# Rotating queries and keys before their norm is applied, and taking squares and weighted copies tile by tile from the accumulation banks, in a decoder step on one Trainium2 core

## The reference, cut to what matters

```python
def rms_norm(x, gain=None):
    x32 = x.astype(jnp.float32)
    y = x32 * lax.rsqrt(jnp.mean(x32 * x32, axis=-1, keepdims=True) + EPS)
    if gain is not None:
        y = y * gain.astype(jnp.float32)
    return y.astype(x.dtype)

def rope_partial(x, pos):
    ...
    x1, x2 = x32[..., :half], x32[..., half:ROPE_DIM]
    out = jnp.concatenate([x1 * cos - x2 * sin, x1 * sin + x2 * cos, x32[..., ROPE_DIM:]], axis=-1)

def qkv_heads(h, pos, w_qkv, q_gain, k_gain):
    qkv = (h @ w_qkv).reshape(Bt, S, N_GROUPS, 3, N_HEADS, HEAD_DIM)
    q = rope_partial(rms_norm(qkv[:, :, :, 0], q_gain), pos)
    k = rope_partial(rms_norm(qkv[:, :, :, 1], k_gain), pos)
    return q, k, qkv[:, :, :, 2]
```

## Time and profile before

| | us |
|---|---|
| median of 3 runs | 2579.95 (2577.85 to 2580.0) |
| the profiled execution's own time | 2578.79 |
| its span, first to last instruction | 2577.0 |
| TensorE matmul busy in it | 2436.4 (95%) |
| VectorE busy | 1443.5 (56%) |
| ScalarE busy | 956.0 (37%) |
| GpSimd busy | 631.1 (24%) |

### The profile page before, as it was taken

The page is one execution under the profiler, slowest core; times in us unless marked ns, Lnnn a source line. Parts: engine busy times, 40 slices in busy tenths (PEclk is TensorE's granted clock), DMA queues, the critical chain, the costliest instruction groups (busy, mean ns, idle before and its releaser), DMA issues.

```text
span 2577.0 us, 51040 instructions
## 1 busy us (share of the span) xinstructions
PE 2436.4 (95%) x19172; PEld 2200.3 (85%) x19172; DVE 1443.5 (56%) x3329; ACT 956.0 (37%) x1564; POOL 631.1 (24%) x445
## 2 busy tenths in 40 slices
PE   7888999999999999999789978899899999999998
PEld 2577888888889999999687345699899999999998
DVE  5674269467878433333534132259988996333333
ACT  3333433333333444444322021254444443444443
POOL 1014457400000222222243000267800001222222
PEclk8899999999999999999899989899999999999999
DMA  6514445544544454554623563344433333544444
GB/s 242 189 69 145 139 164 190 179 164 158 170 165 138 155 182 163 166 168 163 219 99 106 203 240 125 123 142 163 139 130 124 130 130 131 182 166 166 163 164 139
DMA packets 114388, 405.45 MB, mean 157 GB/s; under 512 B 13240, under 2 KB 13368, under 8 KB 113112
## 3 DMA queue, kind: packets, MB, share of 16 engines
q1 hardware_dynamic: 110616, 388.68, 44.6%
q10 hardware_dynamic: 3648, 15.08, 1.5%
HBM read 394.58 MB, written 9.14 MB: 157 GB/s over the span
## 4 chain that ended last, share of the span: by engine, by line
PE 67%; issue 21%; POOL 9%; DVE 1%; ACT 1%; DMA 1%; POOLq 0%; ACTq 0%; DVEq 0%; SPq 0%
PE ps L1254 11%; PE ps L1250 11%; PE ps L1258 11%; POOL ring_lo L1892 8%; PE ps L1113 7%; PE ps L1114 7%; PE ps L1117 7%; PE ps L1185 5%; PE ps L925 2%; PE ps L701 1%; POOL ring_lo L1899 1%; PE ps L705 1%; PE ps L708 1%; PE ps L777 1%; PE ps L935 1%
## 5 line engine op out<-in xcount | busy, mean ns | idle before, releaser
L364 ACT ACTIVATE wt_hi<-ring 128x1024 fp32r<-128x1024 f32 x552 | 580.4, 1051 | 681.3 <-PE ps L1117 408.5
L1841 DVE TENSOR_TENSOR ring_lo<-ring,wt_hi 128x1024 fp32r<-128x1024 f32 x256 | 315.3, 1232 | 494.7 <-ACT wt_hi L364 494.7
L1113 PE MATMUL ps<-split,wt_hi 128*128 128x288 f32 x2048 | 574.2, 306 | 2.8 <-ACT big L415 2.0
L1114 PE MATMUL ps<-split,wt_hi 128*128 128x288 f32 x2048 | 560.9, 298 | 0.0
L1918 POOL TENSOR_TENSOR split<-big,split 128x288 fp32r<-128x288 f32 x256 | 209.7, 819 | 1261.4 <-ACT split L465 664.2
L1113 PEld LDWEIGHTS ps<-split,wt_hi 128*128 128x128 f32 x2048 | 387.4, 189 | 18.6 <-issue 13.3
L1114 PEld LDWEIGHTS ps<-split,wt_hi 128*128 128x128 f32 x2048 | 387.9, 189 | 0.3
L1117 PE MATMUL ps<-split,ring_lo 128*128 128x288 f32 x2048 | 315.4, 296 | 9.8 <-POOL ring_lo L1892 9.5
L1892 POOL TENSOR_TENSOR ring_lo<-ring,wt_hi 128x1024 fp32r<-128x1024 f32 x104 | 283.2, 2731 | 146.6 <-ACT wt_hi L364 146.3
L1250 PE MATMUL ps<-split,wt_hi 128*128 128x288 f32 x2048 | 313.3, 295 | 5.7 <-DVE ada L1559 3.2
L1254 PE MATMUL ps<-split,wt_hi 128*128 128x288 f32 x2048 | 313.8, 295 | 0.0
(11 more groups left out here) (299 smaller groups left out, 2353.8 us busy)
## 6 DMA issues: line engine op xcount, KB each, us to landing
ring<-in_stream SPq DMA_DIRECT2D x680, 512.0 KB, 3.3
big<-in_kc SPq DMA_DIRECT2D x8, 1792.0 KB, 9.1
big<-in_vc SPq DMA_DIRECT2D x14, 1024.0 KB, 5.9
out_qk<-big ACTq DMA_DIRECT2D x1, 3456.0 KB, 13.0
x_spill<-xT ACTq DMA_DIRECT2D x2, 1152.0 KB, 5.0
big<-x_spill ACTq DMA_DIRECT2D x2, 1152.0 KB, 6.0
out_v<-big ACTq DMA_DIRECT2D x1, 1536.0 KB, 15.9
xT<-in_xT SPq DMA_DIRECT2D x1, 1152.0 KB, 11.1
```

Of the source, the lines that this page charges most:

```text
L364: nc.scalar.activation(wt_hi[:, n % 2 if b is None else b], ring[:, n % RING], ACT.Copy).then_inc(S["hi_ready"], 1)
L1113: mm(out, w, h_hi[:, c], start=(c == 0), stop=False)
L1114: mm(out, w, h_lo[:, c], start=False, stop=False)
L1841: TT(ring_lo[:, s], ring[:, s], wt_hi[:, s % 2].bitcast(F32), ALU.subtract)\
```

## The change

The order of the steps is turned round. ScalarE now takes each tile from its bank as soon as it is made, in two instructions: a copy into `qk` that multiplies by the gain on the way, and a square into `asq`. TensorE waits for the square of one tile, not for the copy of a group, before it writes that bank again. The rotation is applied to the weighted copy, before the norm's factor is known; its product with the sines goes into a buffer of its own, `turned_qk`, so that `asq` stays with the squares. The factor is multiplied in last. `rotate` stands behind tile 0 of the next group, `norm` behind tile 1, `spread_out` behind tile 3.

```diff
                     act.wait_ge(S["tile_done"], QK + 4 * gs + m + 1)
-                    if gs < 5 or m < 2:
+                    nc.scalar.activation(qk[:, 4 * gs + m, :], ps[:, m, 0:T], ACT.Copy, scale=(kg if gs % 2 else qg))\
+                       .then_inc(S["aq_copied"], 1)
+                    if gs and m == 0:
+                        high(act, QK + 4 * gs + 2)
+                        act.wait_ge(S["aq_ms"], gs)
+                    nc.scalar.activation(asq[:, m, :], ps[:, m, 0:T], ACT.Square).then_inc(S["aq_sq"], 1)
+                    if (gs < 5 or m < 2) and (gs == 0 or m):
                         high(act, QK + 4 * gs + m + 2)
-                    if gs and m == 0:
+                    if gs and m == 1:
                         qk_root(gs - 1)
-                nc.scalar.activation(qk[:, 4 * gs:4 * gs + 4, :], ps[:, 0:4, 0:T], ACT.Copy)\
-                   .then_inc(S["aq_copied"], 1)
...
             def norm(gs):
-                pe.wait_ge(S["aq_sq"], gs + 1)
-                if gs:
-                    pe.wait_ge(S["aq_done"], gs)
+                pe.wait_ge(S["aq_sq"], 4 * gs + 4)
+                pe.wait_ge(S["aq_turned"], gs + 1)
...
             def rotate(gs):
-                pe.wait_ge(S["aq_qn"], gs + 1)
+                if gs == 0:
+                    pe.wait_ge(S["in_att"], 80)
+                pe.wait_ge(S["aq_copied"], 4 * gs + 4)
+                if gs:
+                    pe.wait_ge(S["aq_done"], gs)
...
             for gs in range(6):
-                if gs:
-                    pe.wait_ge(S["aq_copied"], gs)
                 for m in range(4):
+                    if gs:
+                        pe.wait_ge(S["aq_sq"], 4 * gs + m - 3)
                     qk_tile(4 * gs + m, ps[:, m, 0:T])
                     if gs and m == 0:
+                        rotate(gs - 1)
+                    if gs and m == 1:
                         norm(gs - 1)
-                    if gs and m == 1:
+                    if gs and m == 3:
                         spread_out(gs - 1)
-                    if gs and m == 2:
-                        rotate(gs - 1)
...
-            pe.wait_ge(S["aq_copied"], 6)
+            pe.wait_ge(S["aq_sq"], 24)
...
-            def finish(gs):
+            def turn_qk(gs):
                 q = qk[:, 4 * gs:4 * gs + 4, :]
                 v.wait_ge(S["aq_rot"], gs + 1)
-                own(TT(asq, ps[:, 4:8, 0:T], rope[:, 1].unsqueeze(1).broadcast_to([P, 4, T]), ALU.mult))
+                TT(turned_qk, ps[:, 4:8, 0:T], rope[:, 1].unsqueeze(1).broadcast_to([P, 4, T]), ALU.mult)\
+                    .then_inc(S["aq_turned"], 1)
                 own(TT(q, q, rope[:, 0].unsqueeze(1).broadcast_to([P, 4, T]), ALU.mult))
-                own.settle()
-                TT(q, q, asq, ALU.add).then_inc(S["aq_done"], 1)
+                v.wait_ge(S["aq_turned"], gs + 1)
+                own.settle()
+                own(TT(q, q, turned_qk, ALU.add))
...
                 v.wait_ge(S["aq_sp"], gs + 1)
-                STT(out=q, in0=q, scalar=(kg if gs % 2 else qg), in1=ps[:, 4:8, 0:T], op0=ALU.mult, op1=ALU.mult)\
-                    .then_inc(S["aq_qn"], 1)
-                v.wait_ge(S["aq_qn"], gs + 1)
+                own.settle()
+                TT(q, q, ps[:, 4:8, 0:T], ALU.mult).then_inc(S["aq_done"], 1)
...
             for gs in range(6):
-                if gs:
-                    scale_qk(gs - 1)
-                    finish(gs - 1)
-                    v.wait_ge(S["aq_done"], gs)
-                v.wait_ge(S["aq_copied"], gs + 1)
-                q = qk[:, 4 * gs:4 * gs + 4, :]
-                TT(asq, q, q, ALU.mult).then_inc(S["aq_sq"], 1)
-            scale_qk(5)
-            finish(5)
+                turn_qk(gs)
+                scale_qk(gs)
```

More of the change, by code:

```diff
@@ L259, in build @@
         pt_sb = [x.rearrange("p (e k) -> p e k", e=2) for x in (scratch[:, 3072:4608], rb.take(1536))]
+        ps_at = rb.at
         ps_s = [rb.take(SW), big[:, rope_at:rope_at + SW]]
@@ L263, in build @@
         ptn = [x.rearrange("p (g r) -> p g r", g=3) for x in (rb.take(3 * 128), big[:, end + 7 * 128:end + 10 * 128])]
+        turned_qk = big[:, ps_at:ps_at + 4 * T].rearrange("p (m t) -> p m t", m=4)
         kv_buf = [rb.take(4 * CK) for _ in range(3)]
@@ L272, in build @@
             "qn_ready sc_mm sc_copied gate_in gate_exp sel_ready sel_t idx_ready gb_oh gb_mm gb_mul gb_cp x_out x_in g_zero "
-            "gelu_done w_done aq_copied aq_sq aq_ms aq_sd aq_qn aq_rot aq_done v_copied qz_ready "
+            "gelu_done w_done aq_copied aq_sq aq_ms aq_sd aq_rot aq_turned aq_done v_copied qz_ready "
             "us_mm us_st us_max us_exp us_t us_cpa us_pv us_o us_ot us_nd ss_mm ss_max ss_exp ss_t ss_cp "
@@ L780, in attention_pe @@
                     if g == 0 and s == 0:
+                        rotate(5)
+                    if g == 0 and s == 1:
                         norm(5)
-                    if g == 0 and s == 1:
+                    if g == 0 and s == 2:
                         spread_out(5)
-                    if g == 0 and s == 2:
-                        rotate(5)
                     if g == 1 and s == 0:
```

## The result

The changed kernel takes 2564.31 us in the median of five runs (2558.31 to 2565.29), the kernel before 2579.95 (five runs, 2575.8 to 2580.3). The medians differ by 15.6 us. The ratio over all runs is 0.9936 with a 95% interval of 0.9921 to 0.9952, which is 16.5 us less, between 12.4 and 20.4. The prediction gave 2561, within 2557 to 2566.

The account below looks back on a forecast made before the run. TensorE's five waits for ScalarE's group copy were taken as the bound in the query and key stage. 11.65 + 1.44 + 4.50 + 0.85 = 18.4 us saved; 2560.4 from the profiled execution, 2561.5 from the median, given as 2561, range 2557 to 2566.

Parts of the forecast that it names:

- The bound: Query and key stage: the other engines delay TensorE only by five waits for ScalarE's copy of a group, 10.8 us.
- The boundaries' 11.65 us: At the five group boundaries, the wait for the group's copy goes, 2.33 us each.
- the values' 1.44 us: At the values' start, the first matmul no longer comes late, since `spread_out(4)` covers the last tile's copy and square.
- The falls: Query and key stage: three falls of the clock behind gaps go with the gaps, 1.50 us each, 4.5 us.
- The weight of 0.17 on falls that stay: Rival: one to three falls of the clock stay or appear, 1.50 us each, 2562.5 to 2565.5 us; chance 0.17.
- The order of the small steps: In each group, one tile follows another tile instead of a gap, 13.28 us for 13.45; five times 0.17, 0.85 us won.
- ScalarE's instructions: Per tile, a weighted copy of 0.49 us and a square of 0.41 replace a quarter of a copy; hidden, cost nothing.
- The tight place: Fourth tile's third pass awaits GpSimd, behind ScalarE's conversion queued after `norm`: slack 0.7 us; late split or tables, chance 0.05.
- table load: Rival: ScalarE's square and root in different tables, two loads of 1.283 us a group, 2564 us; given almost nothing.
- VectorE's: After `rotate`, the product with the sines takes 1.36 us, 2.53 at most beside GpSimd, with 1.5 us of slack.
- The sum: Whole kernel: 18.4 us less than the profiled execution.
- "Downstream": Later stages start by no absolute time and move along; they may catch one fall more or less, 1.5 us each way.

Follow-up runs that it names:

- e2: Changed kernel, but TensorE waits at a group's start for all four squares of the group before; median 2560.26 us over six runs, ratio 0.9941.
- e3: Kernel before, with only ScalarE's copy made tile by tile ahead of the conversion, TensorE waiting for one tile's copy; median 2562.09 us, ratio 0.9943.
- e5: Changed kernel with TensorE waiting at each group's start for GpSimd's rest of the second tile; median 2588.06 us over nine runs, ratio 1.0035.
- e1: Changed kernel run again as it was; median 2566.7 us over twelve runs, against 2576.44 over 23 of the kernel before, ratio 0.9954.
- e6: Changed kernel with each square made twice, the extra result unread; stage 101.56 us, one execution of 2564.59 us.
- e7: Changed kernel with each square made three times, the extra results unread; stage 104.47 us, one execution of 2581.21 us.
- second comparison: Changed kernel unaltered, twelve more runs, against 23 of the kernel before; medians 2566.7 and 2576.44 us, ratio 0.9954.
- e8: Changed kernel with GpSimd waiting at the stage's head until VectorE is done with the modulation; median 2561.99 us over six runs, ratio 0.9931.
- e12: Kernel before with the whole group's copy ahead of the conversion, a second profile; one execution of 2567.5 us, beside 2575.67 of the kernel before.
- e4: Kernel before with the whole group's copy moved ahead of the conversion behind the fourth tile; median 2577.68 us over twelve runs, ratio 0.9998.

## Why the prediction was right, point by point

**The bound** was read rightly: TensorE's five waits for the copy were the one thing late in the stage, and they are gone. The boundaries' 11.65 us came in full. Of the values' 1.44 us some 1.2 came: no wait is left there, but the values' first matmul starts 1.94 us behind the start of `spread_out(4)` (1390.90 - 1388.96), where a spread step was taken at 1.72. e2 shows that behind `spread_out` even a wait for all four tiles is covered, as long as ScalarE reads each tile when it is done; e3 shows that the tile-by-tile copies alone would do. The prediction named both in one breath. In e3 the gap goes without the rotation's new place, from which the change has its name.

**The falls** were sized at three times 1.50 us, and they went as expected: no tile behind the first runs at 1.2 GHz in the changed stage, in two profiles. Measured against a gap without a fall, the three slow tiles of before had cost 1.50, 1.54 and 1.53 us. That they belong to the gaps was an inference from one profile; e5 brings them back with gaps, and the four profiles of before have twelve of them, all behind gaps. The weight of 0.17 on falls that stay was not needed for this stage.

**The order of the small steps** was to give 0.17 us a group. A group takes 17.45 us where 17.35 was worked out: the tile between `rotate` and `norm` takes 1329.49 - 1326.00 = 3.49 us, 0.09 more than the 3.40 of the tile before it. The prediction put the 3.37 us of the tile behind a gap down to the gap. But `norm` followed that tile, and in both kernels it starts 1.16 us behind the third pass (1392.88 - 1391.72 before, 1329.49 - 1328.33 here), where another pass or a tile starts 1.07 behind; this 0.09 stays. So 0.5 of the 0.85 us is missing. The first tile of the second group, which has no `spread_out` in front, gives 0.2 us back: 3.19 us in e1 instead of 3.39.

**ScalarE's instructions** were taken at 0.49 and 0.41 us and measured 0.49 to 0.50 and 0.40 to 0.41. The Trainium skill ("ScalarE: Activation LUTs", What ACT_TABLE_LOAD costs) gives about 93 ns for each column operand and an overlap of about as much back to back, and the trace agrees: 0.09 us between the two, and starts 0.29 to 0.40 us apart of instructions that last 0.40 to 0.50. The tight place has 0.76 us of slack where 0.7 was worked out; e6 took 0.6 of it for nothing, and e7 found its end. No table load stands in the stage.

**VectorE's** product of two operands in the main memory took 1.85 to 1.92 us next to GpSimd, under the bound of 2.53, and is covered.

**The sum** was 18.4 us. The stage gave 18.36 against the first profile of before, but 0.3 of that is the quicker first group of that one execution; e1 gives 18.05, and the means of four profiles before (119.29) and two after (101.41) give 17.9. So the fit to 0.1 us is luck, and the fit to half a microsecond is not. The medians moved by 15.6 us, and in the second comparison by 9.7, by its ratio 11.9 us with an interval of 7.7 to 16.0, which leaves out the stage's 18. By their ratios, e2, e3 and e8, whose stages are nearly as short, were 15, 15 and 18 us quicker than the kernel before. What is missing lies outside the stage, as far as the profiled executions show: the rest varies by up to 18 us with its clock, and the stage's start by 9.

**"Downstream"** was the weakest step of the prediction. It asked whether anything later starts by absolute time, and gave a fall more or less, 1.5 us each way; measured is a rest of 1166 to 1185 us. That the first median of 2564.31 stayed within 2557 to 2566 owes something to luck: the twelve runs of e1 have 2566.7, with a kernel before that was itself 3.5 us quicker there. Whether the removal of the gaps makes the later stages slower, or seven profiles are too few, stays open. Four profiles of before have a rest within 0.9 us of each other, which speaks for some link between the stage and what follows, but 23 executions of that kernel differ by 13.7 us; the rests of e3 and e12, 1168.9 and 1167.5 us, speak against a link.

## What to carry to other kernels

Where one engine's copy frees the accumulation banks that TensorE waits for, try that copy in front of the engine's other work, and tile by tile, before anything larger; in e3 that alone made the stage 17.4 us shorter, where the whole change made it 18.4 us shorter, without any new order of the mathematics. The same copy put in front but left whole (e4) made it 9.3 us shorter, and the time of twelve runs no shorter. A stall of TensorE can cost more than its length: the five gaps of 2.3 us cost another 4.6 us of slow clock, while gaps of 1.4 us did not. And where the clock of other stages moves one kernel's time by 20 us, a saving of 1% is judged by the length of its stage in several profiles, not by a median of five.

## What the runs showed of the hardware that was not expected

- Behind twenty gaps of TensorE of 2.3 us (four profiles of before) the clock fell twelve times, behind the ten gaps of 1.4 us (e4, e12) never.
- The number of falls was three in each of the four profiles, though not always at the same gaps.
- In the attention over the prompt, with the same code, the mean granted clock of a 102 us stretch was between 0.74 and 0.88, and the rest of the program between 1166.4 and 1184.6 us long with it. Between e4 and the changed kernel all of these 18 us arise before the norm that follows the attention; from there to the end the fourteen profiles differ by 3.0 us at most.
- VectorE and GpSimd slow each other by who begins first: the same square took 2.53 us when it began 1.0 us into GpSimd's subtraction, and 1.36 when it began 0.09 us ahead of it, while that subtraction then took 3.52 us instead of 2.39 (e3).
